# Pooling by shifted sums on GpSimd, with the channel matrix folded into the input projection

## The reference

```python
h = modulate(rms_norm(x, norm_pre_g), shift, scale)
xa, ga, q, k, v, gb, gm = split_columns(h @ w_in)        # xa: 512 wide
# pool_mixer: 4 groups of 128 channels, windows 2, 4, 8, 16
for g, w in enumerate(POOL_WINDOWS):
    lo = jnp.clip(t - w // 2, 0, L); hi = jnp.clip(t + w // 2, 0, L)
    mean = (P[:, hi, g] - P[:, lo, g]) / (hi - lo)       # P: prefix sums over tokens
    outs.append(mean - xg[:, :, g])
y = einsum('bsgc,gcd->bsgd', pooled, pool_w) * pool_scale
y_a = y * silu(ga)
y_b = windowed_attention(q, k, v, k_ctx, v_ctx, sink) * silu(gb)   # +-128 tokens and 256 context keys
merged = sigmoid(gm_a) * (y_a @ w_branch_a) + sigmoid(gm_b) * (y_b @ w_branch_b)
out = x + gate * rms_norm(merged @ w_out, norm_post_g)
```

## Time and profile before

| | us |
|---|---|
| runs (three) | 2420.18, 2423.65, 2423.89; median 2423.65 |
| profiled execution | 2422.03, span 2420.4 on core 7 |
| TensorE matmuls busy | 2336.0 (97%), 33440 instructions |
| VectorE, ScalarE, GpSimd busy | 1283.9 (53%), 1235.5 (51%), 678.5 (28%) |
| spans of the eight cores | 2410.8 to 2420.4 |

### The profile page before, as it was taken

One profiled execution on the slowest core, in us unless ns is written; L12 is line 12 of the kernel. 1 busy time (PEld: TensorE's weight loads), 2 busy tenths in 40 slices (PEclk: granted clock), 3 DMA queues, 4 the chain that ended last, 5 costly groups with the idle time before them and its releaser, 6 DMA issues.

```text
span 2420.4 us, 83721 instructions; the slowest of 8 cores (2410.8 to 2420.4 us)
## 1 busy us (share of the span) xinstructions
PE 2336.0 (97%) x33440; PEld 1785.9 (74%) x33440; DVE 1283.9 (53%) x3503; ACT 1235.5 (51%) x2375; POOL 678.5 (28%) x677
## 2 busy tenths in 40 slices
PE   6768999999999999999999999999999999999998
PEld 1436877877787787777777778778777877877786
DVE  0424555555555555555554555555555555555553
ACT  0323555555555555555555555555555555555553
POOL 1111323332232333223222223232322323332232
PEclk9889999999999999999999999999999999999999
DMA  8994222212222222222322232223122222322211
GB/s 215 186 175 85 65 68 59 76 59 66 66 64 69 59 76 59 65 67 72 69 76 67 69 64 66 67 59 76 59 67 65 65 67 59 76 58 66 58 48 54
DMA packets 179533, 181.80 MB, mean 75 GB/s; under 512 B 142544, under 2 KB 150864, under 8 KB 176592
## 3 DMA queue, kind: packets, MB, share of 16 engines
q1 hardware_dynamic: 176560, 154.75, 25.0%
q0 software_dynamic: 2592, 21.69, 5.1%
HBM read 126.79 MB, written 33.56 MB: 66 GB/s over the span
## 4 chain that ended last, share of the span: by engine, by line
PE 92%; DMA 3%; POOL 1%; DVE 1%; issue 1%; another core or an unknown queue 1%; ACT 0%; SPq 0%; POOLq 0%; DVEq 0%; ACTq 0%
PE pb L503 35%; PE pb L496 16%; PE pb L708 9%; PE pb L724 9%; PE pb L636 8%; PE pb L662 6%; PE pb L698 5%; PE pb L340 2%; PE pb L598 2%; DMA gg_scr<-s_xr 2%; DMA s_wmf<-w_mod 1%; PE pb L607 1%; POOL s_xr L742 0%; DMA s_hT<-s_xsb 0%
## 5 line engine op out<-in xcount | busy, mean ns | idle before, releaser
L503 PEld LDWEIGHTS pb<-s_hT,s_W 128*128 128x128 bf16 x15360 | 870.4, 98 | 122.8 <-issue 120.8
L503 PE MATMUL pb<-s_hT,s_W 128*128 128x128 bf16 x15360 | 937.6, 219 | 13.3 <-DVE s_Gb L577 6.4
L639 ACT ACTIVATE s_PT<-pb 128x512 bf16<-128x512 f32 x1264 | 651.9, 604 | 295.5 <-PE pb L636 295.5
L496 PE MATMUL pb<-s_W,s_hT 128*128 128x512 bf16 (+1 forms) x2048 | 423.7, 355 | 0.0
L555 DVE TENSOR_TENSOR s_scr<-pb,s_ropet 128x512 f32<-128x512 f32 x256 | 164.9, 686 | 322.3 <-PE pb L503 322.3
L496 PEld LDWEIGHTS pb<-s_W,s_hT 128*128 128x128 bf16 x2048 | 194.1, 99 | 159.4 <-issue 5.3
L560 POOL TENSOR_TENSOR s_qT<-s_scr 128x512 bf16<-128x512 f32 x128 | 160.0, 1271 | 536.0 <-DVE s_scr L555 536.0
L712 POOL TENSOR_TENSOR s_mgT<-s_ub,s_scr 128x512 bf16<-128x512 f32 x128 | 162.6, 1270 | 406.0 <-DVE s_scr L689 406.0
L708 PE MATMUL pb<-s_ybT,s_wmf 128*128 128x128 bf16 x4096 | 249.7, 219 | 2.4 <-issue 2.4
L671 DVE SCALAR_TENSOR_TENSOR s_yb<-pb,s_small,s_Gb 128x64 bf16<-128x64 f32 x1024 | 220.1, 277 | 28.7 <-DVE s_small L668 1.5
L708 PEld LDWEIGHTS pb<-s_ybT,s_wmf 128*128 128x128 bf16 x4096 | 232.4, 98 | 3.0 <-issue 3.0
(11 more groups left out here) (77 smaller groups left out, 2106.1 us busy)
## 6 DMA issues: line engine op xcount, KB each, us to landing
s_xt<-x SPq DMA_DIRECT2D x64, 512.0 KB, 4.0
s_xr<-x SPq DMA_DIRECT2D x64, 512.0 KB, 3.4
y<-s_xr SPq DMA_DIRECT2D x64, 512.0 KB, 2.7
s_W<-w_in POOLq DMA_DIRECT2D x11, 1024.0 KB, 41.3
s_wmf<-w_mod SPq DMA_DIRECT2D x4, 2048.0 KB, 12.3
s_ropet<-rope SPq DMA_DIRECT2D x64, 128.0 KB, 2.0
s_wmf<-w_mod POOLq DMA_DIRECT2D x2, 2048.0 KB, 79.1
s_xt<-ctx SPq DMA_DIRECT2D x4, 512.0 KB, 11.3
```

The costliest lines, as they stand in the source:

```text
L496: E("pe", lambda e, k=k: e.matmul(out=pb[:, c0:c0 + n], lhsT=h[:, k, :], rhs=W[:, wblk, k, c0:c0 + n], start=(k == 0), stop=(k == 7)), rea ...
L503: E("pe", lambda e, c=c, k=k: e.matmul(out=pb[:, c * 128:(c + 1) * 128], lhsT=W[:, wblk, k, c * 128:(c + 1) * 128], rhs=h[:, k, :], start= ...
L639: E("act", lambda e, g=g: e.activation(out=PT[:, jb, g, :], in_=banks[g][0][:, :], func=AF.Exp, scale=0.125), reads=[banks[g][1]], writes= ...
```

## The change

The weights of the pool projection are multiplied with the scaled channel matrix on the chip, once, before the first tile (`fold_pool`: block 1 of `w_in` is loaded transposed into the space of `PT`, 32 matmuls, eight copies into `W`). `P_xa` then gives rows of channels (`feat_block`: 32 matmuls with 128 columns), kept in bf16 with 8 tokens of the neighbours on either side; ScalarE copies the edges over. `pool_sums` on GpSimd adds each row to itself shifted by 1, 2, 4 and 8 tokens (windows 2, 4, 8, 16), and `pool_gate` on VectorE divides, subtracts the token and multiplies with the gate. `pool1`, `pool2`, the band table and its load go.

Also moved: the key block of the next tile is visited fourth and not third; softmax products come behind both merge products and are evacuated in pairs with one reciprocal; the context's own projection stands later; the tanh buffer is doubled, a fifth scratch buffer added, and the output banks stay out of use a little longer.

```diff
-            for blk in range(1, 6):
+            E("pool", lambda e: e.dma_start(out=view(PT, 0, [[1, 4096]]), in_=win_d[1]),
+              writes=[bf(f"PT{j}_{g}") for j in range(2) for g in range(4)], dma_sem=dsem("d_cPT"))
+            for blk in range(2, 6):
                 load_w(blk)
             load_cast(view(maskb, 0, [[1, 256]]), mask_d, "maskb")
-            load_cast(view(band, 0, [[1, 2560]]), band_d, "band")
...
+        def fold_pool():
+            for k in range(8):
+                pb, pbb = next_bank()
+                for g in range(4):
+                    E("pe", lambda e, pb=pb, k=k, g=g: e.matmul(out=pb[:, g * 128:(g + 1) * 128], lhsT=view(PT, g * 1024 + k * 128, [[1, 128]]),
+                                                                rhs=Wp[:, g, :], start=True, stop=True),
...
         def P_xa(t):
...
-            pb, pbb = tok_block(t, 1)
-            E("act", lambda e: e.activation(out=xa[t % NR][:], in_=pb[:, :], func=AF.Copy), reads=[pbb], writes=[bf(f"xa{t % NR}")])
+            pb, pbb = feat_block(t, 1)
...
+            E("act", lambda e: e.activation(out=xa[a][:, :, 8:136], in_=view(pb, 0, [[128, 4], [1, 128]]), func=AF.Copy),
...
+        def pool_sums(t):
...
+            add(sA[:, :, 0:142], x[:, 1:4, 0:142], x[:, 1:4, 1:143], xb, [bf("sA")])
+            add(sF[:, 0, :], x[:, 0, 7:135], x[:, 0, 8:136], xb, [bf("sF0")])
+            add(sB[:, :, 0:140], sA[:, 1:3, 0:140], sA[:, 1:3, 2:142], [bf("sA")], [bf("sB")])
+            add(sF[:, 1, :], sA[:, 0, 6:134], sA[:, 0, 8:136], [bf("sA")], [bf("sF1")])
+            add(sF[:, 2, :], sB[:, 0, 4:132], sB[:, 0, 8:136], [bf("sB")], [bf("sF2")])
+            add(sC[:, 2, 0:136], sB[:, 1, 0:136], sB[:, 1, 4:140], [bf("sB")], [bf("sA")])
+            add(sF[:, 3, :], sC[:, 2, 0:128], sC[:, 2, 8:136], [bf("sA")], [bf("sF3")])
...
+        def pool_gate(t):
...
+            for g, w in enumerate(POOL_WINDOWS):
+                E("dve", lambda e, g=g, w=w: e.scalar_tensor_tensor(out=sF[:, g, :], in0=sF[:, g, :], scalar=1.0 / w, in1=x[:, g, 8:136],
+                                                                   op0=ALU.mult, op1=ALU.subtract),
...
+            E("dve", lambda e: e.tensor_tensor(out=ya[:], in0=view(sF, 0, [[1, 512]]), in1=Ga[:], op=ALU.mult),
...
             out.append(("lat", t % NR, None))
+            out.append(("ctx", 0, None))
             if i < NT - 1:
                 out.append(("lat", (t + 1) % NR, 1))
-            out += [("ctx", 0, None), ("ctx", 1, None)]
+            out.append(("ctx", 1, None))
...
             next(q, None)
+            if hasA:
+                pool_sums(p)
...
             if hasG:
                 u = A_mm(tm, 1)
-            if hasA:
-                pv(p, 0)
-                pv(p, 1)
             if hasG:
                 tm = gm(p - 1, 10)
+                B_mm(tm, 1, u)
...
             if hasA:
-                pv(p, 2)
-                pv(p, 3)
-            if hasG:
-                B_mm(tm, 1, u)
+                pv_pair(p, 0)
+                pv_pair(p, 2)
...
             if hasA:
-                pool1(p)
                 ga(p)
...
-                pool2(p)
+                pool_gate(p)
```

More of the change, by code:

```diff
@@ L504, in feat_cols @@
                                                          start=(k == 0), stop=(k == 7)),
-                      reads=[bf(f"{hn}_{k}"), bf(f"W{wblk}")], writes=[pbb], inc=(k == 7 and c == nch - 1 and last))
+                      reads=[bf(f"{hn}_{k}"), bf(f"W{wblk}" if wblk != 1 else f"W1_{k}")], writes=[pbb], inc=(k == 7 and c == nch - 1 and last))
         def tok_block(t, wblk):
@@ L587, in pool1 @@
-        def pool1(t):
+              reads=[ttb, pbb], writes=[bf("Ga")])
+        def pool_sums(t):
             i = t % NT
-            pb, pbb = next_bank()
-            for g in range(4):
-                terms = []
-                if i > 0:
-                    terms.append(((t - 1) % NR, 5 * g + 3))
-                terms.append((t % NR, 5 * g + (1 if i == 0 else (2 if i == NT - 1 else 0))))
-                if i < NT - 1:
-                    terms.append(((t + 1) % NR, 5 * g + 4))
-                for ti, (rs, mi) in enumerate(terms):
-                    E("pe", lambda e, g=g, rs=rs, mi=mi, ti=ti, nterm=len(terms): e.matmul(
-                        out=pb[:, g * 128:(g + 1) * 128], lhsT=xa[rs][:, g * 128:(g + 1) * 128], rhs=band[:, mi, :],
-                        start=(ti == 0), stop=(ti == nterm - 1)),
-                      reads=[bf(f"xa{rs}"), bf("band")], writes=[pbb], inc=(g == 3 and ti == len(terms) - 1))
-            E("act", lambda e: e.activation(out=pooled[:], in_=pb[:, :], func=AF.Copy), reads=[pbb], writes=[bf("pooled")])
@@ L604, in pool2 @@
-        def pool2(t):
-            pb2, pbb2 = next_bank()
-            for g in range(4):
-                E("pe", lambda e, g=g: e.matmul(out=pb2[:, g * 128:(g + 1) * 128], lhsT=Wp[:, g, :], rhs=pooled[:, g * 128:(g + 1) * 128],
-                                                start=True, stop=True),
-                  reads=[bf("pooled"), bf("Wp")], writes=[pbb2], inc=(g == 3))
-            E("dve", lambda e: e.tensor_tensor(out=ya[:], in0=pb2[:, :], in1=Ga[:], op=ALU.mult),
-              reads=[pbb2, bf("Ga")], writes=[bf("ya")])
+            x = xa[t % 3]
@@ new lines, in pool_sums @@
+            add(sF[:, 1, :], sA[:, 0, 6:134], sA[:, 0, 8:136], [bf("sA")], [bf("sF1")])
+            add(sF[:, 2, :], sB[:, 0, 4:132], sB[:, 0, 8:136], [bf("sB")], [bf("sF2")])
+            add(sC[:, 2, 0:136], sB[:, 1, 0:136], sB[:, 1, 4:140], [bf("sB")], [bf("sA")])
+            add(sF[:, 3, :], sC[:, 2, 0:128], sC[:, 2, 8:136], [bf("sA")], [bf("sF3")])
+            fb = [bf(f"sF{g}") for g in range(4)]
+            for side, c0 in ((0, 0), (1, 120)):
+                if i == (0 if side == 0 else NT - 1):
+                    E("pool", lambda e, side=side, c0=c0: e.tensor_tensor(out=sF[:, :, c0:c0 + 8], in0=sF[:, :, c0:c0 + 8], in1=edge[:, side, :, :],
+                                                                         op=ALU.mult), reads=fb + [bf("edge")], writes=fb)
@@ L766, in start_loads, with flush_out @@
             next_load()
+        late = []
+        HOLD = 40
+        def flush_out():
+            while late:
+                t, obs = late.pop()
+                out_evac(t, obs)
+                for _, ob in obs:
+                    ob.touch += HOLD
+                if (t + 1) % NT == 0 and t + 1 < TT:
+                    load_gg((t + 1) // NT)
         def period(p):
@@ L928, in rows @@
         return f(a.reshape(-1, 128, a.shape[1]).transpose(1, 0, 2).reshape(128, -1))
+    w_blocks = blocks(w_all)
+    w_blocks[1] = rows(f(xa_c.T))
     b_mod = f(b_mod)[0]
     shared = {
-        "w_in": blocks(w_all),
+        "w_in": w_blocks,
         "w_a": rows(f(w_branch_a)[0]),
@@ L943, in _prep_shared @@
         "rope": rope_tables(L),
[L944 removed]
+        "edge": edge_tables(),
         "mask": mask_tables(),
```

129 lines of the change are left out of this document (82 added, 47 removed).

## The result

The changed kernel takes 2332.39 us (median of four runs, 2332.26 to 2335.12) against 2422.7 for the kernel before in the same session: a ratio of 0.9631, 95% interval 0.9615 to 0.9648. Forecast were 2337 and a range of 2322 to 2392. The profiled execution took 2332.26 us, its span 2330.7 on core 0.

What follows compares the result with a forecast made beforehand. TensorE was taken as the bound, its period falling from 35.30 to 33.99 us with GpSimd's loop hidden. Terms 77.3 + 1.8 + 2.4 + 3.8 = 85.3 us off 2422.03 gave 2336.7, stated as 2337, range 2322 to 2392.

Steps and rivals of the forecast that it cites:

- the projection's form: TensorE's pool projection: 32 matmuls of 128 columns instead of 8 of 512, forecast to add 0.05 us a period.
- the second sample's first tile: TensorE's 2.4 us wait for new keys goes as their visit moves back; 0.6 more from changed matmuls.
- The band and pool-weight terms: TensorE, per five-block period: 12 band matmuls removed, 0.66 us, and 4 with the pool weight, 0.22 us.
- the 0.48: TensorE's third scores visit: 0.48 us a period lost where keys just arrive, forecast to go when it moves fourth.
- The start: Queue of casting loads: without the band table's 640 KB, TensorE's wait ends 3.8 us earlier; bounds 0 and 6.
- The bound of 6: Upper bound on the start's 3.8 us, if the band load moves its fp32 source at a lower rate.
- X: Time of the seven sums on GpSimd up to the merged-branch addition: taken 5.3 us, bounds 4.2 and 7.4.
- the limit: Loop over GpSimd and VectorE to the next key projection: hidden as long as X stays under 5.5 us.
- The slower rival's 6.9: GpSimd becomes the bound at TensorE's key projection: slower from X = 6.9, 2455 us at X = 7.4; chance 0.09 slower.
- That the 0.48 stays: Rival: another visit meets its keys just in time, 28 us less gain, 2365; 0.23 shared with loop showing slightly.
- that the new form costs 81 and 131 ns: Rival: TensorE's projection by the skill page's prices, another 1.5 us a period, 2430 us; chance 0.01.
- that the loop over GpSimd shows or binds: Rivals: X above 5.5 delays TensorE's key projection; 0.23 shared with lost time kept, 0.06 showing more, 0.09 slower, 0.04 same.

Runs made afterwards that it cites:

- the sixteen matmuls: Changed kernel with 12 and 4 unread 128-column matmuls put back at the band's and pool weight's old places: 2390.72 us, ratio 0.987.
- the load: Changed kernel with an unused 640 KB casting load put back at the band table's place in the queue: 2335.77 us, ratio 0.9644.

## Why the prediction was right, step by step

The parts add up on the chip too. The visit alone is worth 33.7 us, the sixteen matmuls 58.3, the load 3.4; less 62 x 0.05 = 3.1 for the projection's form they make 92.3, and 90.3 were measured. These totals carry the scatter of the start: the fourth tile's first visit, with which the long stretch below begins, comes at 232.4 us on average over the changed kernel's cores, and at 234.9 in its second profiled execution. The 60 periods of the stretch are free of it (means of the eight cores): 2127.5 us before, 2094.2 with the visit moved alone, 2046.8 after, 2099.4 with the sixteen back. So the visit is 33.3 and the matmuls 52.7, less 60 x 0.05 = 3.0 together 83.0, where 80.7 were measured.

**The period.** Forecast 35.30 to 33.99. Over a long stretch the first visits of a period, of the kernel before and of the one after, are

```profile
241.72 0.61 PE L636 MATMUL pb<-s_qT,s_kT 32*128 32x512 bf16 x8
...
1054.21 0.61 PE L636 MATMUL pb<-s_qT,s_kT 32*128 32x512 bf16 x8
```

```profile
234.86 0.61 PE L674 MATMUL pb<-s_qT,s_kT 32*128 32x512 bf16 x8
...
1050.54 0.61 PE L674 MATMUL pb<-s_qT,s_kT 32*128 32x512 bf16 x8
```

23 periods before, 35.33 each, and 24 after, 33.99 each. So a period gains 1.34 and not 1.31; 59 of them 79.0 where 77.3 stood. The chosen period was 0.03 short of the mean, 1.7 of the 5 us between forecast and measurement; the second sample's first tile (below) is 0.5, and most of the rest lies in the start. The band and pool-weight terms are confirmed at 56 ns a matmul; the 0.48 at 0.48 alone and 0.46 with the rest of the change in place.

**A price on the projection's form.** The rebuilt projection and the sixteen matmuls are at 56 ns. The Trainium skill's page "TensorE: Matmul & The Clock Gate", section "Back-to-back issue gap", has 81 ns for such a stream; by it sixteen matmuls would have added 62 x 1.3 = 80 us, an estimate, where 58.3 were measured. The runs do not agree with it. The prediction also used the page's prices on one side only: by 81 ns the sixteen matmuls that go would have been worth 1.30 us a period, an estimate, and with them the change would have kept 0.2 us a period, not nothing.

**The second sample's first tile** was forecast to gain 2.4 + 0.6; it gained 3.5 (37.52 to 34.01 us between first visits).

**The start.** 3.8 were forecast, with bounds 0 and 6. On the slowest cores the wait for the last casting loads ends 5.24 us earlier, but 2.6 on average over the eight, and the load put back moves the average by 3.1. So 3.8 was about right or a little high. The bound of 6 does not follow from its reason: the fp32 source, twice the 640 KB, takes 7.6 us at the 173 GB/s of the stretch. How much of the load's 3 us is left at the end of the kernel is not shown.

**The range.** Its terms reach down to 2335 only (6 us at the start in place of 3.8). The measured 2332.39 lies below that, and in the range thanks to a margin for which the prediction names no term.

**X, the sums.** Taken 5.3, measured 4.40. The contention's price was right: beside a mask the first sum gains 457 ns and the second 454, 0.91 us where 0.95 stood. The uncontended price was wrong: 389 ns for 128 elements, 642 for 280 and 888 for 426 lie on 176 + 1.67 per element, and the rows used, 456 and 1275, gave 183 + 2.13. With the measured line 1354 elements and seven instructions make 3.5, and 3.5 + 0.91 = 4.4. It cost the forecast nothing, because X was under the limit either way.

How that contention works the prediction had wrong, though its price came out. The two masks one by one, beside the query additions and sums shown above:

```profile
387.58 1.56 DVE L687 TENSOR_TENSOR s_PT<-s_PT,s_maskb 128x1024 bf16<-128x1024 bf16 x1
...
389.05 1.38 DVE L687 TENSOR_TENSOR s_PT<-s_PT,s_maskb 128x1024 bf16<-128x1024 bf16 x1
```

GpSimd's query additions end at 388.58. The first mask ends at 389.14, its own 0.68 us from 388.46 on; the first sum at 389.88, its own 0.89 from 389.00 on; the second mask at 390.43, 0.68 from 389.75 on; the second sum at 390.69, 0.39 from 390.30 on. So each waits until the other engine's instruction is done but for some 0.13 us, and then takes its own time. The Trainium skill's page "SBUF — State Buffer" (on the shared port pair) says that one holds the pair of ports for its whole instruction and the other blocks; the trace agrees, the 0.13 us of hand-over apart. The prediction took it that the rule fits only in part, because both partners grow; they both grow because they wait in turn. And a sum that comes to a mask already at work loses only the rest of it, 0.46 us, so two masks cost 0.91 and not the 1.4 of two whole ones.

**The room.** The chain behind the sums came out as added up: from the end of the second query block (383.11 + 1.96) to the last feature, at 404.64, it is 19.57 us, X + 15.2 where X + 15.3 stood. The limit was put at X = 5.5. At X = 5.26 a plain period is unchanged, with 0.3 us left at the features, so the limit lies at about 5.56 there; at X = 8.10 the period grows by 2.84, 0.3 more than 8.10 - 5.56, the price of matmuls that meet their operands one by one. That place, the key projection, was named; the bank wait ahead of it, worth 1.11 of the 2.84, was not. So the room in a plain period of the changed kernel is 1.2 us, and not the 0.2 that the forecast gave: the loop was less close to showing than the forecast had it, because X was smaller. Some periods have less room, which the forecast did not separate: one addition more costs some 7 us in 11 of the 60. The slower rival's 6.9 is 1.6 times the measured X; with the sums done twice, at 8.10, the kernel is indeed slower.

**The rivals.** That the 0.48 stays was excluded by the form's 78 ns; that the new form costs 81 and 131 ns by the period; that the loop over GpSimd shows or binds, by the period of 33.99 here and by the same period with one addition more. The other moves of the change (softmax products later and in pairs, the context's projection later, the buffers, the output banks) were not tried alone. In the 60 periods the parts that were tried make 83.0 of 80.7 us, so no gain is left that would need them.
